# Weight sums of Strassen products: GpSimd adds in place of accumulating transfers

## The reference

```
x += 0.5 * SwiGLU(RMSNorm(x));  x += Mixer(RMSNorm(x));  x += 0.5 * SwiGLU(RMSNorm(x))
swiglu(x, wg, wu, wd) = (silu(x @ wg) * (x @ wu)) @ wd        # wg, wu: 1024 x 2816, wd: 2816 x 1024
```

## Time and profile before

| what | value |
|---|---|
| median of three runs | 1840.48 us (1838.13 to 1842.96) |
| profiled execution | 1838.35 us |
| its span | 1836.5 us |
| TensorE busy | 1823.1 us, 99% of the span |
| VectorE, ScalarE, GpSimd busy | 74%, 45%, 16% |
| granted TensorE clock | 1.00 in every slice |

### The profile page before, as it was taken

One profiled execution on the slowest core, in us unless ns is written; L12 is line 12 of the kernel. 1 busy time (PEld: TensorE's weight loads), 2 busy tenths in 40 slices (PEclk: granted clock), 3 DMA queues, 4 the chain that ended last, 5 costly groups with the idle time before them and its releaser, 6 DMA issues.

```text
span 1836.5 us, 26251 instructions
## 1 busy us (share of the span) xinstructions
PE 1823.1 (99%) x9996; PEld 1559.7 (85%) x9996; DVE 1350.3 (74%) x2120; ACT 827.4 (45%) x1357; POOL 292.1 (16%) x239
## 2 busy tenths in 40 slices
PE   9999999999999999999999999999999999999999
PEld 7888988978888988989889898897777788989889
DVE  7686865978866768768777686687787666858656
ACT  6343433643343434435434344355666543434433
POOL 0310401223102204012030130111111003104011
PEclk9999999999999999999999999999999999999999
DMA  5244236632222322347323222762222232322356
GB/s 188 77 142 120 92 115 174 165 109 69 99 97 94 114 92 92 115 149 196 115 69 126 99 97 93 193 155 90 74 66 86 68 116 75 133 92 92 115 168 154
DMA packets 80027, 210.20 MB, mean 114 GB/s; under 512 B 15176, under 2 KB 28137, under 8 KB 79914
## 3 DMA queue, kind: packets, MB, share of 16 engines
q1 hardware_dynamic: 57088, 182.48, 28.8%
q0 software_dynamic: 9216, 16.78, 5.2%
q10 hardware_dynamic: 13610, 9.41, 1.9%
HBM read 189.76 MB, written 3.93 MB: 105 GB/s over the span
## 4 chain that ended last, share of the span: by engine, by line
PE 90%; DVE 3%; DMA 3%; issue 2%; ACT 1%; POOL 0%; SPq 0%; ACTq 0%; POOLq 0%; DVEq 0%
PE bank L1514 25%; PE bank L1516 24%; PE bank L1515 24%; PE bank L1465 5%; PE bank L1468 4%; PE bank L1469 4%; DMA rest<-rest 1%; PE bank L1727 1%; PE bank L1718 1%; DVE wlr L508 0%; DMA raw_area<-in_ffn_w_down 0%; DMA icnt<-in_c_count 0%; PE bank L1743 0%; ACT whr L499 0%; PE bank L1707 0%
## 5 line engine op out<-in xcount | busy, mean ns | idle before, releaser
L1514 PE MATMUL bank<-xh,whr 128*128 128x512 f32 x1408 | 550.2, 391 | 1.8 <-DVE xl L939 1.0
L1515 PE MATMUL bank<-xl,whr 128*128 128x512 f32 x1408 | 547.9, 389 | 0.0
L1516 PE MATMUL bank<-xh,wlr 128*128 128x512 f32 x1408 | 547.9, 389 | 0.0
L476 ACT ACTIVATE whr<-rest 128x512 fp32r<-128x512 f32 (+1 forms) x445 | 273.0, 616 | 456.4 <-PE bank L1516 445.7
L485 DVE TENSOR_TENSOR wlr<-rest,whr 128x512 fp32r<-128x512 f32 (+1 forms) x445 | 322.8, 729 | 121.8 <-ACT whr L476 119.1
L1514 PE MATMUL bank<-hsh,whr 128*128 128x256 f32 x1232 | 349.3, 283 | 0.9 <-DVE x L1236 0.8
L1515 PE MATMUL bank<-hsl,whr 128*128 128x256 f32 x1232 | 348.6, 283 | 0.0
L1516 PE MATMUL bank<-hsh,wlr 128*128 128x256 f32 x1232 | 348.6, 283 | 0.0
L1514 PEld LDWEIGHTS bank<-xh,whr 128*128 128x128 f32 x1408 | 264.3, 188 | 59.1 <-issue 2.1
L1516 PEld LDWEIGHTS bank<-xh,wlr 128*128 128x128 f32 x1408 | 264.3, 188 | 55.4
L1515 PEld LDWEIGHTS bank<-xl,whr 128*128 128x128 f32 x1408 | 264.3, 188 | 55.3 <-issue 1.0
(11 more groups left out here) (199 smaller groups left out, 2126.9 us busy)
## 6 DMA issues: line engine op xcount, KB each, us to landing
rest<-in_ffn_w_gate SPq DMA_DIRECT2D x61, 512.0 KB, 3.8
rest<-in_ffn_w_up SPq DMA_DIRECT2D x61, 512.0 KB, 4.6
rest<-in_ffn_w_down SPq DMA_DIRECT2D x54, 512.0 KB, 4.7
raw_area<-in_ffn_w_gate SPq DMA_DIRECT2D x26, 512.0 KB, 3.8
raw_area<-in_ffn_w_up SPq DMA_DIRECT2D x26, 512.0 KB, 4.7
raw_area<-in_ffn_w_down SPq DMA_DIRECT2D x26, 512.0 KB, 4.6
raw_area<-in_w_qkv SPq DMA_DIRECT2D x24, 512.0 KB, 3.5
rest<-rest POOLq DMA_DIRECT2D x38, 256.0 KB, 4.7
```

The costliest lines, as they stand in the source:

```text
L476: act.activation(whr[:, at:at + st.kb, :].rearrange("p k c -> p (k c)"), weights(st, buf)[:, 0, :], ACT.Copy).then_inc(high, 1)
L1514: pe.matmul(out, whr[:, at, :], hi, start=start, stop=False, skip_group_check=onto)
L1515: pe.matmul(out, whr[:, at, :], lo, start=False, stop=False, skip_group_check=onto)
L1516: return pe.matmul(out, wlr[:, at, :], hi, start=False, stop=stop, skip_group_check=onto)
```

## The change

GpSimd makes the four sums of every down step with adds, in third parts as in the others. The accumulating transfers, their semaphores, and the two transfers from HBM that brought copies are dropped. GpSimd's order becomes plain: for each down step, wait for both halves of its load, then four adds. Steps are numbered through all three parts for the waits on `sums`.

```diff
--- before.py
+++ after.py
@@ -101,7 +101,6 @@
         self.buf, self.sums, self.place, self.into, self.fresh, self.reads = buf, sums, place, into, fresh, reads
 
 
-POOL_PARTS = 2
 H_B11, H_T1, H_B21, H_B22, H_T3, H_T2, H_T4 = range(7)
 PRODUCTS = (Product(B_A11, None, H_B11, "X", True, 0), Product(B_S1, 0, H_T1, "Z", True, 0),
             Product(B_A12, None, H_B21, "Y", True, 0), Product(B_S2, 1, H_T2, "X", False, 1),
@@ -133,8 +132,7 @@
         self.first, self.half = PARTS[part]
         self.kb = self.half
         self.d = (2 * pair, 2 * pair + 1)
-        self.by_transfer = part >= POOL_PARTS
-        self.number = KD // 2 * (POOL_PARTS * ffn + part if not self.by_transfer else ffn) + pair
+        self.number = KD // 2 * (len(PARTS) * ffn + part) + pair
         self.hpair = KF // 2 * ffn + self.first // 2
         self.ends = part == len(PARTS) - 1
         self.bank = ({"Y": 4, "Z": 5, "X": 6, "W": 7} if pair % 2 == 0 else {"Y": 0, "Z": 1, "X": 2, "W": 3})
@@ -173,7 +171,7 @@
 def plan():
     phases = [Run("run0", (0,), 2), Phase("w_in", KH, 4), Phase("w_out", 2, 4), Run("run1", (1, 2), 1),
               Phase("qkv", PAIRS, 3), Phase("w_o", 2, 4), Run("run2", (3,), 2)]
-    unit, group, uses, set_uses, set_downs = 0, 0, [0] * 4, [0] * RAW_SETS, [0] * RAW_SETS
+    unit, group, uses, set_uses = 0, 0, [0] * 4, [0] * RAW_SETS
     for n, ph in enumerate(phases):
         ph.unit0, ph.group0, ph.uses0 = unit, group, list(uses)
         unit += ph.units
@@ -182,8 +180,6 @@
             for st in ph.steps:
                 set_uses[st.set] += 1
                 st.loads = set_uses[st.set]
-                set_downs[st.set] += st.kind == "down" and st.by_transfer
-                st.copies = set_downs[st.set]
         else:
             for s in range(ph.per):
                 uses[s] += ph.iters
@@ -304,8 +300,6 @@
         first_in = [sem(f"first_in{s}") for s in range(2)]
         first_gate, first_hidden = sem("first_gate"), sem("first_hidden")
         sums = sem("sums")
-        sum_s1, sum_s2, sum_s3, sum_s4 = sem("sum_s1"), sem("sum_s2"), sem("sum_s3"), sem("sum_s4")
-        copy_in = [sem(f"copy_in{s}") for s in range(RAW_SETS)]
         step_in = [[sem(f"step_in{s}{half}") for half in range(2)] for s in range(RAW_SETS)]
         mix_in, toep_in, braw_in = sem("mix_in"), sem("toep_in"), sem("braw_in")
         high, low, unit_done, evac = sem("high"), sem("low"), sem("unit_done"), sem("evac")
@@ -381,13 +375,6 @@
                 sp.dma_start(weights(st, B_A21 if half else B_A11, 2), src.rearrange("p (b c) -> p b c", b=2))\
                   .then_inc(step_in[st.set][half], 16)
 
-            def bring_copies(st):
-                size = st.half * P
-                sp.dma_start(weights(st, B_S1)[:, 0, :],
-                             wd[st.ffn, st.d[1], :, st.first * P:st.first * P + size]).then_inc(copy_in[st.set], 16)
-                src = wd[st.ffn, st.d[0], :, st.first * P:st.first * P + 2 * size]
-                sp.dma_start(weights(st, B_S2, 2), src.rearrange("p (b c) -> p b c", b=2)).then_inc(copy_in[st.set], 16)
-
             def run(ph):
                 for st in ph.steps:
                     if ph.before is None and st.t == 0:
@@ -409,8 +396,6 @@
                             sp.wait_ge(low, ph.unit0 - 1 + LOW_CREDIT)
                     for half in range(2):
                         bring_half(st, half)
-                    if st.kind == "down" and st.by_transfer:
-                        bring_copies(st)
 
             def load(ph, i):
                 for j in range(ph.per):
@@ -462,11 +447,7 @@
                 else:
                     act.wait_ge(step_in[st.set][half], 16 * st.loads)
             else:
-                which = PRODUCTS[n].sums
-                if st.by_transfer:
-                    act.wait_ge((sum_s1, sum_s2, sum_s3, sum_s4)[which], 16 * (st.number + 1))
-                else:
-                    act.wait_ge(sums, SUMS * st.number + (1, 2, 4, 3)[which])
+                act.wait_ge(sums, SUMS * st.number + (1, 2, 4, 3)[PRODUCTS[n].sums])
             if v >= 4:
                 act.wait_ge(unit_done, run.unit0 + v - 3 + UNIT_CREDIT)
             elif run.before:
@@ -1831,43 +1812,23 @@
         @block.gpsimd
         def _(pool):
 
-            def onto(st, dst, src, landed):
-                pool.dma_start(weights(st, dst)[:, 0, :], weights(st, src)[:, 0, :], accum_op=ALU.add).then_inc(landed, 16)
-
             of = lambda st, buf: weights(st, buf)[:, 0, :]
 
-            def first_sums(st):
+            def pair_sums(st):
 
                 for half in range(2):
                     pool.wait_ge(step_in[st.set][half], 16 * st.loads)
-                if not st.by_transfer:
-                    pool.tensor_tensor(of(st, B_S1), of(st, B_A21), of(st, B_A22), ALU.add).then_inc(sums, 1)
-                    pool.wait_ge(sums, SUMS * st.number + 1)
-                    pool.tensor_tensor(of(st, B_S2), of(st, B_S1), of(st, B_A11), ALU.add).then_inc(sums, 1)
-                    pool.wait_ge(sums, SUMS * st.number + 2)
-                    pool.tensor_tensor(of(st, B_S4), of(st, B_A12), of(st, B_S2), ALU.add).then_inc(sums, 1)
-                    pool.tensor_tensor(of(st, B_S3), of(st, B_A11), of(st, B_A21), ALU.add).then_inc(sums, 1)
-                    return
-                pool.wait_ge(copy_in[st.set], 32 * st.copies)
-                onto(st, B_S1, B_A22, sum_s1)
-                onto(st, B_S3, B_A11, sum_s3)
-
-            def second_sums(st):
-                if not st.by_transfer:
-                    return
-                pool.wait_ge(sum_s1, 16 * (st.number + 1))
-                onto(st, B_S2, B_S1, sum_s2)
-                pool.wait_ge(sum_s2, 16 * (st.number + 1))
-                onto(st, B_S4, B_S2, sum_s4)
+                pool.tensor_tensor(of(st, B_S1), of(st, B_A21), of(st, B_A22), ALU.add).then_inc(sums, 1)
+                pool.wait_ge(sums, SUMS * st.number + 1)
+                pool.tensor_tensor(of(st, B_S2), of(st, B_S1), of(st, B_A11), ALU.add).then_inc(sums, 1)
+                pool.wait_ge(sums, SUMS * st.number + 2)
+                pool.tensor_tensor(of(st, B_S4), of(st, B_A12), of(st, B_S2), ALU.add).then_inc(sums, 1)
+                pool.tensor_tensor(of(st, B_S3), of(st, B_A11), of(st, B_A21), ALU.add).then_inc(sums, 1)
 
             def ffn_run(ph):
-                downs = [st for st in ph.steps if st.kind == "down"]
-                for n, st in enumerate(downs):
-                    if st.pair == 0:
-                        first_sums(st)
-                    second_sums(st)
-                    if st.pair + 1 < KD // 2:
-                        first_sums(downs[n + 1])
+                for st in ph.steps:
+                    if st.kind == "down":
+                        pair_sums(st)
 
             ffn_run(by["run0"])
```

## The result

The changed kernel takes 1852.99 us (median of four runs, 1851.89 to 1853.58), the kernel before 1839.92 us beside it (again a median of four): a ratio of 1.0066, with a 95% interval of 1.0054 to 1.0079. It is slower by some 13 us. The forecast was 1849.0 us in a range of 1839.5 to 1855.0, so the time lies inside it and the direction is right. The profiled execution took 1851.89 us, its span is 1850.1 us, 13.6 us more than before.

A forecast was written before the change was run, and what follows sets the result against it. TensorE's matmul stream was taken to bound the kernel, busy 1823.1 of 1836.5 us. The terms 2.8 + 6.9 - 1.1 = 8.6 us gave 1849.0 us, 0.47% slower, in a range of 1839.5 to 1855.0.

The forecast's parts named there:

- Exclusion between an add and a VectorE operation with two SBUF operands: GpSimd adds and VectorE operations reading two SBUF operands exclude each other; each of four adds holds VectorE 0.75 to 1.1 us.
- First step: First step of four third parts: third pair's adds delay hidden sums, TensorE waits 0.7 us each, 2.8 us (1.6 to 4.0).
- these cost nothing: First two pairs' adds fall into the up steps ahead of the part, where VectorE has idle time: no cost.
- block 4's wait for the second result: First step of a third part: block 4 needs VectorE's add from the second result, with 0.15 us of room.
- Second step: Second step of three third parts with a norm: fourth pair's adds delay two results, 3 x 2.3 = 6.9 us (3.3 to 10.5).
- the middle walk: Second step, adds from 334.2 us behind the first split, `xl` held: waits of 0.4 and 1.9, 2.3 us.
- the upper walk: Second step, adds from 333.6 us with `xl` held: waits of 1.5 and 2.0, 3.5 us.
- Third and fourth steps: Last two steps of a third part: no adds fall there, so no cost.
- Gain of the transfers: Removed transfers in 16 steps: worth the third FFN's wait, 1.1 us (nothing to 1.7).
- Absorbed: Rival: adds beginning over about 3 us later, behind the step's second result, cost nothing; 0 to -1.7 us, some 1839.4; chance 0.28.
- Nothing absorbed: Rival: VectorE carries all four delays of 1.1 us into TensorE; 16.5 us, 1857 us; chance 0.06.
- ScalarE waiting for sums: Rival: the adds become a wait of their own on ScalarE, priced as the absorbed rival; chance 0.02.

The follow-up runs named there:

- the late adds above: Changed kernel, with GpSimd holding the third and fourth pair's adds of third parts until VectorE has taken the step's second result; 1852.31 us.
- the floor kernel: Changed kernel, with GpSimd zero fills in place of the third and fourth pair's adds in third parts, those sums left out; 1836.73 us, ratio 0.9977.
- the kernel with the shorter chain: Kernel before, with S4 taking A11 and then S1 in place of S2, in all four pairs of third parts; 1837.44 us, ratio 0.9981.

## Why the prediction was right, and where its terms were off

- **What bounds the kernel.** Right: 13.5 of the 13.6 us by which the span grew are lost by TensorE in third parts.
- **Exclusion between an add and a VectorE operation with two SBUF operands.** Right, in both kinds of operation, and shown by taking it away: fills in place of adds bring VectorE back to 0.68 us and the loss of a third part to 0.2 us or less.
- **First step, 4 x 0.7 us forecast, 4 x 1.5 measured (5.9 us).** This is the term that was mis-sized most; it lies above its own upper bound of 4.0. The step that failed is "these cost nothing" about the first two pairs' adds: they don't stop TensorE, but they hold the splits on which the third pair's load is issued. I had checked what waits for the adds, and not what is issued behind the operations that they delay. It made 0.5 us per FFN; the other 0.3 is the middle taken between two bounds where the upper one held. The path was wrong as well: I took block 4's wait for the second result, with 0.15 us of room, and TensorE waited for the low parts of the hidden sums, in blocks 2 and 3. That the room of the second of them is 0.13 us, nearly the same, is luck. (Four adds 1.38 us apart from 317.8 on end at 323.3, not at 323.25; that changes little.)
- **Second step, 3 x 2.3 forecast, 2.39, 3.49 and 2.39 measured (8.3 us).** Right: two of the FFNs came out as the middle walk and one as the upper walk of the list. Where the adds start against the split at the head of the step decides between them, as the walks said. FFN 3 lost nothing there, as forecast.
- **Third and fourth steps, nothing forecast, 1.3 us measured.** A part of it is 0.28 and 0.27 us in the third steps of FFNs 0 and 2, behind second steps that lost 2.39. The 0.43 us of FFN 3 follow a second step that lost nothing; there ScalarE makes no split for 3.37 us around the issue of an output that waits for a late result, and VectorE waits 0.69 us for the split after next, as with the late adds above. The 0.14 us in the last step are there in the kernel before too.
- **Gain of the transfers, 1.1 us forecast, 3 to 4 us measured.** The waits of one execution priced it. The kernel before moves between 1837 and 1846 us from run to run, the floor kernel between 1836.2 and 1837.9: the profiled execution, 2.1 us under the median of three, lost 1.2 us to a late chain once. That the chain is late more often in slower runs is not shown, since no trace of one was taken; the kernel with the shorter chain, 1836.8 to 1838.9, speaks for it. I carried the 2.1 us to the forecast as a constant; by that run most of them were the cost of the very thing that the change removes.
- **The sum.** Adds forecast at 9.7 us and measured at 16.3 (changed kernel against floor), transfers at 1.1 and measured at 4.0: the errors have opposite effects, so that 1849.0 us came within 4 us of 1853.0. That it came so near is in part luck.
- **The rivals.** Absorbed: no, and not under its own condition either: adds that were kept behind the second result lost 2.3 us one step later. Nothing absorbed, 17.6 us for the adds and 1857 in all: nearer than I gave it, since the adds by themselves cost 16.3. ScalarE waiting for sums: no, TensorE's losses in the first two steps end with operations of VectorE, and ScalarE's waits in third parts name a sum in FFN 2 alone (2.1 us).

What stays open: why the chain of transfers ends late in some executions and in time in others was not tried; the shorter chain shows only that it no longer matters once S4 is issued earlier. It also takes away GpSimd's wait for S2 ahead of the next pair's first transfers, and these two are not told apart. Nor is the spread of the kernel before wholly explained: of its 64 runs beside the experiments, 13 have a mean granted clock of 0.998 or 0.999, the six slowest (1843.7 to 1845.8 us) among them, while all runs of the changed kernel and of the floor have 1.000. Whether late transfers led to that is not shown.

## What to carry to other kernels

An engine that is free is not a free engine: before work moves to GpSimd, ask what VectorE does in those microseconds, and count the operations with two SBUF operands that have no slack. A delay on VectorE also delays what is issued behind it, so the place of the next load has to be worked out anew. And don't price a removed transfer by the waits of one profile alone: look at the spread of the runs too.

## What the runs show of the hardware

GpSimd's fills (128x512, 0.5 us each) run beside VectorE's two-operand operations without holding them, its copies (one operand read, about 0.6 us) hold them for 0.08 to 0.41 us, its adds (two operands, 1.3 us) for 0.75 to 1.1 us. In the records a held operation and the add overlap a little: the split of 0.67 us ends 0.54 us after the add.
